# A weight ring of 16 chunks in place of 12, four windows in place of six, and the residual stream parked in DRAM, in a diffusion block with 32 experts

## The chip, the core and the metric

One core of one Trainium2 chip. Its engines are PE (TensorE, matmuls), DVE (VectorE), ACT (ScalarE), POOL (GpSimd) and SP (SyncE, here only an issuer of DMAs). The metric is the device time of one execution in microseconds.

## The reference, cut to what matters

A layer of a diffusion backbone over 512 tokens of 1024 channels: a mixer (Fourier heads and a gated linear recurrence), a gated residual, and then experts. Each token goes to 4 of 32 experts, each of which is a clamped SwiGLU with three float32 matrices of 1024 x 1024 (12.6 MB):

```python
logits = (hf @ w_router) + b_router
top_val, top_idx = lax.top_k(logits, TOP_K)          # 4 of 32
gates = jax.nn.softmax(top_val, axis=-1)
...
gu = xb @ w_gu[e] + b_gu[e]                           # 1024 -> 2048
gt = jnp.minimum(gu[:, :D_FF], SWIGLU_LIMIT)
up = jnp.clip(gu[:, D_FF:], -SWIGLU_LIMIT, SWIGLU_LIMIT)
act = (up + 1) * (gt * jax.nn.sigmoid(SWIGLU_ALPHA * gt))
out = act @ w_down[e] + b_down[e]                     # 1024 -> 1024
...
x = x + gt_f * moe_ffn(...)
return rmsnorm(x, g_final)
```

## The kernel before

All weights are float32 and are read once. The mixer and the router run up to about 310 us; then the experts run one after the other, each in one or more *items* of 64 token slots (`M`). The number of items of an expert follows from how many tokens chose it; for these inputs 32 experts make 45 items. The experts are sorted by their number of tokens and then put in a fixed order that spreads the big ones (`CST["place"]`): one of the eight biggest, then three smaller ones. An expert's number in this text is its place in that order, from 0, and items are counted from 0 too. Experts 0 to 31 have 2, 1, 2, 1, 2, 1, 1, 1, 3, 1, 1, 1, 2, 1, 1, 1, 4, 1, 2, 1, 2, 1, 1, 1, 2, 1, 1, 1, 2, 1, 1, 1 items. The table of items is worked out on the chip, so the loops over items take their numbers from registers: each engine has a loop of up to 63 turns (`NI`), of which those behind the last item do nothing.

The weights of an expert are 12 *chunks* (`NCH`) of 8 KB a partition, 1 MB each: 0 to 7 for gate and up, 8 to 11 for down. They go two steps:

1. SP loads chunk `c` of an expert into slot `c` of `ring` (`load_chunk`), when the chunk of the expert before has been copied out of that slot in that expert's last item (`wait_moved`). All of SP's loads stand in one queue. Chunks 0 to 7 are two DMAs each (L314), 8 to 11 one (L317).
2. In every item, each chunk is copied from the ring to one of the *windows*, which are typed for the matmul; window `c % NW`, with `NW` = 6. DVE copies chunks 0 to 5, 8 and 9 (`move`, L998), ACT 6, 7, 10 and 11 (`move`, L733). A copy waits until the chunk has landed (`w_loaded_c`) and until PE has used the chunk that lay in the window before (`slot_used`).

PE takes the chunks in order: `gate_up` (L1447) for 0 to 7, `down` (L1459) for 8 to 11; each is eight matmul instructions in the trace. An item opens with two bias matmuls (L1439). Between them stand transposes of the activations (L1469), of the gathered tokens of the next item (L1428) and small ones. DVE's turn for item `b` is: read the registers, pick the tokens of item `b + 2`, SwiGLU of the first half, numbers for the gather, copy 8, SwiGLU of the second half, copy 9, and then the copies 0 to 5 of item `b + 1`, which are waited for as PE frees the windows. ACT's turn: sigmoid, copies 6 and 7, a copy of activations, sigmoid, copy 10, activations, copy 11, and the output.

`xl` holds the residual stream (2 MB, 16 KB a partition) in SBUF from the mixer to the end. Behind the last item the sums of the experts' outputs are read back (`y_sb`), gated, added to `xl`, normalised and stored.

Of the kernel before, what the change touches and what calls it, by code (L numbers as in the profile page):

```python
# [5 lines left out]
F32 = mybir.dt.float32  # L6
# [4 lines left out]
ALU = mybir.AluOpType  # L11
# [3 lines left out]
P = 128  # L15
D = 1024
# [24 lines left out]
NW = 6  # L41
# [56 lines left out]
def build(nc, x, ctx, w_mod, b_mod, w_in, w_fourier, rg_w_a, rg_w_x, w_out, w_router, b_router,  # L98
          w_gate_up, bias_rows, w_down, g_norm_ffn, g_final, cols, cst, dft, out):
    h_dram = nc.dram_tensor("h_rows", (NL, D), F32, kind="Internal").ap()  # L100
    y_dram = nc.dram_tensor("y_rows", (NL * CG, YW), F32, kind="Internal").ap()

    with ExitStack() as stack:
# [107 lines left out]
        ring = at("ring", [P, NCH, CK, 2, HF], SLOT[0])  # L211
        window = [at(f"window_{i}", [P, CK, 2, HF], w) for i, w in enumerate((ZD, ZD + 8 * KB, ZD + 16 * KB, ZD + 24 * KB, ZA + 16 * KB, ZB))]
# [3 lines left out]
        gfin = at("gfin", [P, D], SLOT[3])  # L216
# [10 lines left out]
        o_sb = at("o_sb", [P, TL, D], SLOT[1])  # L227
        junk3 = at("junk3", [P, D], SLOT[2])
# [80 lines left out]
        def load_chunk(sp, c, e):  # L309
            h, k = c // 4, c % 4 * CK  # L310
            if h < 2:
                for g in range(2):
                    n0 = g * FF + h * HF
                    sp.dma_start(ring[:, c, :, g, :], wgu_v[e, :, k:k + CK, n0:n0 + HF]).then_inc(w_ld[c], 16)  # L314
            else:
                k = (c - 8) * CK
                sp.dma_start(ring[:, c, :, :, :].rearrange("p k g n -> p k (g n)"), wd_v[e, :, k:k + CK, :]).then_inc(w_ld[c], 16)  # L317

        def landed_at(c):
            return 32 if c < 8 else 16  # L320

# [35 lines left out]
        def _(sp):  # L357
# [44 lines left out]
            load_chunk(sp, 6, 0)  # L402
            load_chunk(sp, 7, 0)
# [3 lines left out]
            for c in range(4):  # L407
                load_chunk(sp, c, 0)
# [4 lines left out]
            load_chunk(sp, 4, 0)  # L413
            load_chunk(sp, 5, 0)
            sp.wait_ge(S["lg_done"], TL)
            load_chunk(sp, 10, 0)
            load_chunk(sp, 11, 0)
            sp.wait_ge(S["h_stored"], 16 * TL)
            sp.wait_ge(S["gathered"], 16)
            load_chunk(sp, 8, 0)  # L420
            load_chunk(sp, 9, 0)
# [23 lines left out]
            sp.wait_ge(S["stored"], 16 * TL)  # L445
# [115 lines left out]
        def _(act):  # L561
# [167 lines left out]
            def move(c, p, b):  # L729
                act.wait_ge(w_ld[c], landed_at(c) * p + landed_at(c))  # L730
                act.wait_ge(S["slot_used"], NCH * b + c - NW + 1)
                act.nop(nofuse=True)
                A(window[c % NW][:, :, :, :], ring[:, c, :, :, :], ACT.Copy).then_inc(S["moved_by_act"], 1)  # L733

# [25 lines left out]
            def square_out(t):  # L760
                act.wait_ge(S["x_out"], t + 1)
                if t:
                    act.wait_ge(S["ssq_out"], t)
                A(junk3[:, :], xl[:, t, :], ACT.Square, accum_out=ss[:, t:t + 1]).then_inc(S["ssq_out"], 1)
# [11 lines left out]
        def _(dve):  # L776
# [318 lines left out]
            dve.wait_ge(S["begin_done"], 1)  # L1095
            link(V.tensor_copy(place[:, 0:1], ps[0:NE, 4, 0:1]))
# [5 lines left out]
            V.tensor_scalar(table[:, 2 * NI:3 * NI], active[:, :], place[:, 3:4], None, ALU.mult)  # L1102
# [12 lines left out]
            V.memset(item_p[:, NI:], 0)  # L1115
# [6 lines left out]
            V.tensor_copy(item_p[:, 0:NI], ps[:, 5, 2 * NI:3 * NI])  # L1122
# [60 lines left out]
            dve.wait_ge(S["ld_gnf"], 32)  # L1183

            def add_y(t):
# [5 lines left out]
                V.tensor_tensor(xl[:, t, :], xl[:, t, :], y_sb[:, t, :], ALU.add).then_inc(S["x_out"], 1)  # L1191
# [5 lines left out]
            def scaled(t):  # L1197
                dve.wait_ge(S["rt_out"], t + 1)
                link(V.reciprocal(rsf[:, 1, t:t + 1], rsf[:, 1, t:t + 1]))
                V.scalar_tensor_tensor(o_sb[:, t, :], xl[:, t, :], rsf[:, 1, t:t + 1], gfin[:, :], ALU.mult, ALU.mult).then_inc(S["out_ready"], 1)  # L1200
# [337 lines left out]
```

## Time and profile before

| | |
|---|---|
| median of 3 runs | 1547.96 us (1547.79 to 1549.3) |
| profiled execution: its time | 1548.7 us |
| profiled execution: its span | 1546.8 us |
| busy: PE, DVE, ACT, POOL | 1352.8, 904.4, 639.3, 249.4 us |
| DMA from and to HBM | 463.07 MB read, 18.35 MB written |
| mean granted TensorE clock | 0.959 |

The times are of whole executions; the profile is of one of them, and its span leaves out what lies around the first and the last recorded event. Busy times are sums over the span: they don't say which engine sets the pace at a given place. That is read from stages, where one resource is full and another waits, and from the rows of the timeline, whose first two columns are start and duration in us. In brackets stand the idle time of the engine before the row and what ended it.

### The profile page before, as it was taken

Reading aid. Unit: us, or ns where it says so; the run is one execution under the profiler, and the core shown is the slowest. Engines: PE = TensorE matmul, PEld = TensorE weight load, DVE = VectorE, ACT = ScalarE, POOL = GpSimd, SP = SyncE. Lnnn points to the kernel's source line nnn. Section 1 sums busy time; section 2 is a strip of 40 time slices with the busy share of each in tenths; the row PEclk is TensorE's granted clock in tenths of the full one; section 3 lists DMA queues with packets and bytes.
Section 4 is the critical chain, followed back from the end, with each engine's and each line's share of the span. In section 5 each row is a group of like instructions: output and inputs, shape, how many; then the busy total and the mean of one; then the engine's idle time right before and its main releaser. Section 6 shows DMA issues by size and latency. Waiting matters only on the chain.

```text
span 1546.8 us, 23063 instructions
## 1 busy us (share of the span) xinstructions
PE 1352.8 (87%) x6259; PEld 538.8 (35%) x6259; DVE 904.4 (58%) x1452; ACT 639.3 (41%) x720; POOL 249.4 (16%) x156
## 2 busy tenths in 40 slices
PE   4798999489999987999789879999999779979981
PEld 2586567333333322333223223333333223323320
DVE  2999786855565544655456445656555456446546
ACT  3434552234354434444244434544445335335432
POOL 1741143211111101011001101111110011100101
PEclk9799999689999999999999999999999999999996
DMA  9656132739999999399999991699999999999993
GB/s 379 235 211 224 62 109 76 271 128 374 355 383 336 379 383 388 110 381 383 379 364 383 388 375 24 237 384 342 385 339 383 381 364 373 381 387 346 385 377 123
DMA packets 207171, 474.36 MB, mean 307 GB/s; under 512 B 18481, under 2 KB 18993, under 8 KB 206129
## 3 DMA queue, kind: packets, MB, share of 16 engines
q1 hardware_dynamic: 196322, 455.24, 79.6%
q0 software_dynamic: 10832, 18.90, 5.4%
q8 instruction: 9, 0.15, 0.0%
q14 instruction: 8, 0.07, 0.0%
HBM read 463.07 MB, written 18.35 MB: 311 GB/s over the span
## 4 chain that ended last, share of the span: by engine, by line
PE 34%; SPq 29%; DVE 15%; DMA 11%; issue 7%; ACT 3%; DVEq 1%; POOL 0%; ACTq 0%; POOLq 0%
SPq L314 22%; PE ps L1447 21%; PE ps L1459 7%; DMA ring<-in_w_down 6%; SPq L317 4%; DVE bc L845 4%; DMA ring<-in_w_gate_up 2%; DVE window L998 2%; DMA wm<-in_w_mod 2%; ACT window L733 2%; PE ps L1439 1%; PE ps L1325 1%; PE ps L1428 1%; DVE cv L861 1%; PE ps L1317 1%
## 5 line engine op out<-in xcount | busy, mean ns | idle before, releaser
L1447 PE MATMUL ps<-window,xT 128*64 128x512 f32 x2880 | 658.6, 605 | 45.9 <-DVE window L998 39.7
L998 DVE COPY window<-ring 128x2048 f32<-128x2048 f32 x366 | 438.1, 1226 | 211.8 <-DMA ring<-in_w_gate_up 167.8
L1459 PE MATMUL ps<-window,aT 128*64 128x512 f32 x1440 | 341.1, 603 | 20.9 <-DVE window L998 11.0
L733 ACT ACTIVATE window<-ring 128x2048 f32<-128x2048 f32 x180 | 337.9, 1900 | 48.5 <-DMA ring<-in_w_down 45.4
L1447 PEld LDWEIGHTS ps<-window,xT 128*64 128x64 f32 x2880 | 196.3, 138 | 438.7 <-issue 339.1
L727 ACT ACTIVATE sg<-gb 128x256 f32<-128x256 f32 x90 | 37.5, 417 | 491.8 <-DVE gb L1135 491.8
L540 POOL DMA_INDIRECT y_rows<-osb,idx_c x46 | 85.7, 1863 | 624.2 <-ACT osb L723 609.5
L1135 DVE TENSOR_SCALAR gb<-ps 128x256 f32<-128x256 f32 x90 | 38.1, 424 | 249.6 <-PE ps L1447 249.5
L1459 PEld LDWEIGHTS ps<-window,aT 128*64 128x64 f32 x1440 | 90.5, 136 | 178.0 <-issue 131.0
L527 POOL DMA_INDIRECT xg<-h_rows,idx_n x46 | 54.4, 1183 | 469.7 <-DVE idx_n L1028 469.7
L723 ACT ACTIVATE osb<-ps,gate_c 128x512 f32<-128x512 f32 x46 | 31.7, 689 | 112.3 <-PE ps L1459 111.7
L745 ACT ACT_TABLE_LOAD x45 | 57.7, 1283 | 12.2 <-issue 12.0
L1469 PE MATMUL ps<-csb,ab 128*128 128x128 f32 x180 | 40.3, 306 | 23.4 <-DVE ab L1142 23.4
L1439 PE MATMUL ps<-bias_w,pick 128*128 128x512 f32 x135 | 56.1, 470 | 0.7 <-ACT xT L716 0.7
L1469 PEld LDWEIGHTS ps<-csb,ab 128*128 128x128 f32 x180 | 18.4, 143 | 97.1 <-DVE ab L1142 69.5
L1013 DVE COPY metab<-meta 128x20 bf16 (+1 forms) x47 | 8.4, 178 | 70.5 <-issue 70.2
L1439 PEld LDWEIGHTS ps<-bias_w,pick 128*128 128x128 f32 x135 | 22.0, 190 | 73.1 <-issue 72.3
L1265 PE MATMUL ps<-hT_l_hi,win_hi 128*128 128x512 f32 x96 | 38.9, 405 | 6.3 <-DVE hT_l_lo L832 6.3
L716 ACT ACTIVATE xT<-ps 128x512 f32<-128x512 f32 x46 | 27.2, 591 | 33.5 <-PE ps L1428 33.5
L1428 PEld LDWEIGHTS ps<-csb,xg 64*128 64x128 f32 x368 | 26.8, 140 | 40.7 <-issue 40.7
L1142 DVE TENSOR_TENSOR ab<-ub,sg 128x256 f32<-128x256 f32 x90 | 38.3, 425 | 3.1
L1139 DVE SCALAR_TENSOR_TENSOR ub<-ub,gb 128x256 f32<-128x256 f32 x90 | 38.2, 425 | 3.1
(278 smaller groups left out, 1207.7 us busy)
## 6 DMA issues: line engine op xcount, KB each, us to landing
ring<-in_w_gate_up SPq DMA_DIRECT2D x512, 512.0 KB, 11.8
ring<-in_w_down SPq DMA_DIRECT2D x128, 1024.0 KB, 13.6
wm<-in_w_mod SPq DMA_DIRECT2D x4, 2048.0 KB, 21.5
wm_a<-in_w_mod SPq DMA_DIRECT2D x4, 2048.0 KB, 9.0
wm_b<-in_w_mod SPq DMA_DIRECT2D x4, 2048.0 KB, 8.7
win<-in_w_in SPq DMA_DIRECT2D x3, 2048.0 KB, 20.1
x_in<-in_x SPq DMA_DIRECT2D x1, 2048.0 KB, 10.4
wo_f<-in_w_out SPq DMA_DIRECT2D x1, 2048.0 KB, 7.5
```

Of the source, the lines that this page charges most:

```text
L314: sp.dma_start(ring[:, c, :, g, :], wgu_v[e, :, k:k + CK, n0:n0 + HF]).then_inc(w_ld[c], 16)
L317: sp.dma_start(ring[:, c, :, :, :].rearrange("p k g n -> p k (g n)"), wd_v[e, :, k:k + CK, :]).then_inc(w_ld[c], 16)
L527: pool.indirect_dma_start(xg[0:M, :], None, h_dram, bass.IndirectOffsetOnAxis(ap=idx_n[0:M, 0:1], axis=0), bounds_check=last_row, oob_is_e ...
L540: pool.indirect_dma_start(y_dram, bass.IndirectOffsetOnAxis(ap=idx_c[:, 0:1], axis=0), osb[:, :], None, bounds_check=last_part, oob_is_err ...
L733: A(window[c % NW][:, :, :, :], ring[:, c, :, :, :], ACT.Copy).then_inc(S["moved_by_act"], 1)
L745: A(table_kept[:, :], ones[:, 0:1], ACT.Sigmoid)
L845: ins = V.scalar_tensor_tensor(Z, W[:, k, :], csil[:, k, 0:1], Z, ALU.mult, ALU.add)
L998: V.tensor_copy(window[c % NW][:, :, :, :], ring[:, c, :, :, :]).then_inc(S["moved_by_dve"], 1)
L1439: return MMUL(ps[:, bank, :], pick[:, :], bias_w[:, bank * CH:(bank + 1) * CH], start=True, stop=False)
L1447: last = MMUL(ps[M * j:M * (j + 1), h, :].rearrange("m (g n) -> m g n", g=2), xT[:, k, :], window[c % NW][:, k % CK, :, j * GW:(j + 1) * G ...
L1459: last = MMUL(ps[M * y:M * (y + 1), 2, :], aT[:, h, i, M * j:M * (j + 1)], window[c % NW][:, k % CK, y, :], start=False, stop=(h == 1 and ...
L1469: last = nc.tensor.transpose(ps[:, 3, h * GW + i * P:h * GW + (i + 1) * P], ab[:, i * P:(i + 1) * P], ident)
```

## The change

The ring gets 16 slots (`NR`). Chunk `c` of expert `i` lies in slot `(12 i + c) mod 16`, a pattern that repeats after four experts (`PERIOD`), so SP's loop is written out for four experts and DVE and ACT work out the slot in a register (`ring_chunk`). The four further slots lie where `xl` and two of the six windows were. So the windows are four, DVE's copies 4 and 5 move from the end of an item's turn to the beginning of the next, and `xl` is stored to DRAM (`x2_dram`) once the first gather is done and loaded again (`x2`) when the second last expert has been copied out. SP also waits, before each load, that the load of the same chunk of the expert before has landed.

```diff
-NW = 6
+NW = 4
+NR = 16
+PERIOD = 4
...
-        def load_chunk(sp, c, e):
+        def load_chunk(sp, c, e, p):
             h, k = c // 4, c % 4 * CK
+            s = (NCH * p + c) % NR
...
+        def ring_chunk(c, p):
+            return ring[:, bass.ds((p * NCH + c) & (NR - 1), 1), :, :, :].rearrange("p s k g n -> p (s k) g n")
...
+            for t in range(TL):
+                sp.dma_start(x2_dram[t * P:(t + 1) * P, :], xl[:, t, :]).then_inc(S["stored"], 16)
+            load_chunk(sp, 8, 0, 0)
+            load_chunk(sp, 9, 0, 0)
...
-            with sp.Fori(1, NE) as i:
+            def load_expert(i, p, ahead, ahead_of_last):
                 e = sp.value_load(order_i[0:1, bass.ds(i, 1)], min_val=0, max_val=NE - 1)
-                before = sp.value_load(before_i[0:1, bass.ds(i, 1)], min_val=0, max_val=NI)
                 for c in range(NCH):
-                    wait_moved(sp, c, before)
+                    if c >= NR - NCH:
+                        wait_moved(sp, c - (NR - NCH), ahead)
+                    elif ahead_of_last is not None:
+                        wait_moved(sp, c + 2 * NCH - NR, ahead_of_last)
                     sp.nop(nofuse=True)
-                    load_chunk(sp, c, e)
-            sp.wait_ge(S["slot_used"], NCH * n)
+                    sp.wait_ge(w_ld[c], landed_at(c) * i)
+                    sp.nop(nofuse=True)
+                    load_chunk(sp, c, e, p)
+
+            sp.wait_ge(S["stored"], 16 * TL)
+            last = None
+            for p in range(1, PERIOD):
+                ahead = last_item_ahead_of(p)
+                load_expert(p, p, ahead, last)
+                last = ahead
+            with sp.Fori(1, NE // PERIOD) as r:
+                last = last_item_ahead_of(r * PERIOD - 1)
+                for p in range(PERIOD):
+                    ahead = last_item_ahead_of(r * PERIOD + p)
+                    load_expert(r * PERIOD + p, p, ahead, last)
+                    last = ahead
+            last = last_item_ahead_of(NE - 1)
+            wait_moved(sp, 9, last)
             sp.nop(nofuse=True)
-            sp.wait_ge(S["moved_by_dve"], len(BY_DVE) * n + NW)
+            wait_moved(sp, 11, last)
             sp.nop(nofuse=True)
+            load(x2[:, :, :], rows(x2_dram), "ld_x")
             load(gfin[:, :], g_final.partition_broadcast(P), "ld_gnf")
...
-                V.tensor_copy(window[c % NW][:, :, :, :], ring[:, c, :, :, :]).then_inc(S["moved_by_dve"], 1)
+                V.tensor_copy(window[c % NW][:, :, :, :], ring_chunk(c, p)).then_inc(S["moved_by_dve"], 1)
...
-            for c in range(4, NW):
-                move(c, 0)
-
...
                     def first_of_next(c):
-                        dve.wait_ge(S["slot_used"], NCH * b + NW + c + 1)
+                        dve.wait_ge(S["slot_used"], NCH * b + NCH + c - NW + 1)
                         move(c, p_next)
 
+                    second(4)
+                    second(5)
                     dve.wait_ge(S["meta_done"], b + 2)
                     pick_tokens(b + 2, e)
```

The rest of the diff gives `x2` the place of `xl` behind the experts, moves `gfin`, `o_sb` and `junk3`, puts one small DVE instruction into the table's making, and lets the entry behind the last item name the last expert. Below stand instructions in their order on an engine, with the line and the semaphores each waits for (`window_135` to `window_140` are windows 0 to 5).

DVE at the end of an item, before: copies 2 to 5 of the next item into the windows, and the jump back.

```order
L998 COPY window_137<-ring 128x2048 [waits w_loaded_2,slot_used]
L1162 REGISTER_ALU
L998 COPY window_138<-ring 128x2048 [waits w_loaded_3,slot_used]
L1162 REGISTER_ALU
L998 COPY window_139<-ring 128x2048 [waits w_loaded_4,slot_used]
L1162 REGISTER_ALU
L998 COPY window_140<-ring 128x2048 [waits w_loaded_5,slot_used]
L1152 UNCONDITIONAL_BRANCH
L1151 REGISTER_ALU
L1151 COMPARE_AND_BRANCH
```

DVE at the beginning of an item's turn, after: what stands now between the register reads and the token pick; L1188 and L1030 are the wait and the copy of chunks 4 and 5.

```order
L1029 ISA [waits slot_used]
L1030 ISA [waits w_loaded_4]
L1030 REGISTER_ALU
L1030 ISA
L1030 COPY window_135<-ring 128x2048
L1188 REGISTER_ALU
L1030 REGISTER_ALU [waits w_loaded_5,slot_used]
L1030 REGISTER_ALU
L1030 ISA
L1030 COPY window_136<-ring 128x2048
L1045 ISA [waits meta_done]
L1045 COPY metab<-meta 128x20
```

Copies 4 and 5 have moved across the loop's turn, stand ahead of the token pick and of the SwiGLU, and each has register instructions in front.

SP in the loop over experts, before: the first chunk of an expert and the wait of the second.

```order
L326 ISA
L314 ISA [waits moved_by_dve]
L314 DMA ring<-in_w_gate_up 128x2x512
L314 ISA
L314 DMA ring<-in_w_gate_up 128x2x512
L326 REGISTER_ALU
L314 ISA [waits moved_by_dve]
```

SP in the same place, after: the first chunk of the first of four experts (L446 is the index of the expert), and the second.

```order
L334 ISA
L446 REGISTER_ALU [waits moved_by_dve]
L319 ISA [waits w_loaded_0]
L319 DMA ring<-in_w_gate_up 128x2x512
L319 ISA
L319 DMA ring<-in_w_gate_up 128x2x512
L334 REGISTER_ALU
L319 ISA [waits moved_by_dve,w_loaded_1]
L319 DMA ring<-in_w_gate_up 128x2x512
L319 ISA
L319 DMA ring<-in_w_gate_up 128x2x512
L336 ISA
```

The wait for a copy now asks for chunks 8 and 9 of the expert two places back (`moved_by_dve`), and a second wait, for the landing of the same chunk of the expert before (`w_loaded_0`, `w_loaded_1`), has come with it.

## Rows read from the trace of the kernel before

**Rows 1.** By stage: busy us (count) of PE, PEld, DVE, ACT, POOL; clock, DMA share, GB/s.

```profile
485.00:627.00 142.00, 125.91 (x589) 40.45 (x587) 73.41 (x122) 57.09 (x61) 15.05 (x10) 0.99 1.02 369
...
627.00:650.00 23.00, 22.57 (x105) 7.24 (x103) 12.15 (x24) 12.28 (x13) 2.83 (x2) 1.00 0.10 14
...
650.00:792.00 142.00, 126.03 (x591) 40.52 (x589) 74.58 (x123) 56.48 (x61) 15.95 (x10) 0.99 1.03 371
...
792.00:930.00 138.00, 123.57 (x575) 39.59 (x571) 69.81 (x120) 56.81 (x60) 15.50 (x10) 0.99 1.03 375
...
930.00:978.00 48.00, 47.04 (x221) 15.51 (x222) 26.98 (x48) 24.20 (x26) 5.63 (x4) 1.00 0.11 17
...
1403.00:1509.00 106.00, 98.55 (x464) 32.32 (x460) 57.05 (x97) 46.22 (x51) 11.76 (x8) 0.98 1.00 367
```

**Rows 2.** Timeline of PE over one item (start us, us, what).

```profile
1031.30 0.74 PE L1439 MATMUL ps<-bias_w,pick 128*128 128x512 f32 x2
...
1032.06 10.52 PE L1447 MATMUL ps<-window,xT 128*64 128x512 f32 x48
...
1055.54 0.73 PE L1439 MATMUL ps<-bias_w,pick 128*128 128x512 f32 x2
```

**Rows 3.** Timeline of PE: the row that opens an item, at four of the five slow stretches.

```profile
562.42 0.73 PE L1439 MATMUL ps<-bias_w,pick 128*128 128x512 f32 x2
...
630.54 0.74 PE L1439 MATMUL ps<-bias_w,pick 128*128 128x512 f32 x2
...
868.22 0.74 PE L1439 MATMUL ps<-bias_w,pick 128*128 128x512 f32 x2
...
934.33 0.73 PE L1439 MATMUL ps<-bias_w,pick 128*128 128x512 f32 x2
...
1201.11 0.73 PE L1439 MATMUL ps<-bias_w,pick 128*128 128x512 f32 x2
...
1269.32 0.74 PE L1439 MATMUL ps<-bias_w,pick 128*128 128x512 f32 x2
...
1342.05 0.73 PE L1439 MATMUL ps<-bias_w,pick 128*128 128x512 f32 x2
...
1407.75 0.73 PE L1439 MATMUL ps<-bias_w,pick 128*128 128x512 f32 x2
```

**Rows 4.** Timeline of SP's queue: weight loads issued (start us, us, what, count).

```profile
315.21 0.88 SPq L317 DMA_DIRECT2D ring<-in_w_down  x2
...
339.16 17.65 SPq L314 DMA_DIRECT2D ring<-in_w_gate_up  x16
...
485.23 17.99 SPq L314 DMA_DIRECT2D ring<-in_w_gate_up  x16
...
789.24 19.77 SPq L314 DMA_DIRECT2D ring<-in_w_gate_up  x16
```

**Rows 5.** Timeline of ACT: the copy of expert 8's chunk 11.

```profile
626.71 1.91 ACT L733 ACTIVATE window<-ring 128x2048 f32<-128x2048 f32 x1 [0.29 <-DMA ring<-in_w_down]
```

**Rows 6.** DMA issues by tile: count, KB each, median us from issue to landing.

```profile
ring<-in_w_gate_up SPq DMA_DIRECT2D x512, 512.0 KB, 11.8
...
xl<-in_x SPq DMA_DIRECT2D x1, 2048.0 KB, 7.8
```

**Rows 7.** Costliest groups of the page: DVE's copies.

```profile
L998 DVE COPY window<-ring 128x2048 f32<-128x2048 f32 x366 | 438.1, 1226 | 211.8 <-DMA ring<-in_w_gate_up 167.8
```

**Rows 8.** What PE waited for, 317 to 1514 us: total, times, longest.

```profile
PE ps L1459 <- DVE window L998: 11.0, 45, 0.3
```

**Rows 9.** Timeline of DVE from the end of one item to the next.

```profile
1055.66 1.23 DVE L998 COPY window<-ring 128x2048 f32<-128x2048 f32 x1 [0.39 <-PE ps L1459]
1058.47 0.17 DVE L1013 COPY metab<-meta 128x20 bf16 x1 [1.58 <-issue]
```

**Rows 10.** Timeline of DVE behind the last item.

```profile
1526.29 3.06 DVE L1188 TENSOR_TENSOR y_sb<-y_sb,bc 128x1024 f32<-128x1024 f32 x1 [11.35 <-issue]
...
1533.79 1.23 DVE L1191 TENSOR_TENSOR xl<-xl,y_sb 128x1024 f32<-128x1024 f32 x1
```

More of the change, by code:

```diff
@@ L100, in build @@
     h_dram = nc.dram_tensor("h_rows", (NL, D), F32, kind="Internal").ap()
+    x2_dram = nc.dram_tensor("x2_rows", (NL, D), F32, kind="Internal").ap()
     y_dram = nc.dram_tensor("y_rows", (NL * CG, YW), F32, kind="Internal").ap()
@@ L209, in build @@
         table = at("table", [NE, 3 * NI + 2 * NE], RA + 8 * KB)
-        ring = at("ring", [P, NCH, CK, 2, HF], SLOT[0])
-        window = [at(f"window_{i}", [P, CK, 2, HF], w) for i, w in enumerate((ZD, ZD + 8 * KB, ZD + 16 * KB, ZD + 24 * KB, ZA + 16 * KB, ZB))]
+        ring = at("ring", [P, NR, CK, 2, HF], SLOT[0])
+        window = [at(f"window_{i}", [P, CK, 2, HF], w) for i, w in enumerate((ZD, ZD + 8 * KB, ZD + 16 * KB, ZD + 24 * KB))]
         xg = at("xg", [P, D], ZB + 16 * KB)
@@ L215, in build @@
         bias_w = at("bias_w", [P, 3 * CH], ZB + 8 * KB, F32R)
-        gfin = at("gfin", [P, D], SLOT[3])
+        gfin = at("gfin", [P, D], ZX + 8 * KB)
         osb = at("osb", [P, YW], ZB + 20 * KB)
@@ L226, in build @@
         y_sb = at("y_sb", [P, TL, D], SLOT[0])
-        o_sb = at("o_sb", [P, TL, D], SLOT[1])
-        junk3 = at("junk3", [P, D], SLOT[2])
+        x2 = at("x2", [P, TL, D], SLOT[1])
+        o_sb = at("o_sb", [P, TL, D], SLOT[2])
+        junk3 = at("junk3", [P, D], SLOT[3])
         zero = at("zero", [P, D], ZB + 18 * KB)
@@ L313, in load_chunk @@
                     n0 = g * FF + h * HF
-                    sp.dma_start(ring[:, c, :, g, :], wgu_v[e, :, k:k + CK, n0:n0 + HF]).then_inc(w_ld[c], 16)
+                    sp.dma_start(ring[:, s, :, g, :], wgu_v[e, :, k:k + CK, n0:n0 + HF]).then_inc(w_ld[c], 16)
             else:
                 k = (c - 8) * CK
-                sp.dma_start(ring[:, c, :, :, :].rearrange("p k g n -> p k (g n)"), wd_v[e, :, k:k + CK, :]).then_inc(w_ld[c], 16)
+                sp.dma_start(ring[:, s, :, :, :].rearrange("p k g n -> p k (g n)"), wd_v[e, :, k:k + CK, :]).then_inc(w_ld[c], 16)
         def landed_at(c):
             return 32 if c < 8 else 16
+        def ring_chunk(c, p):
+            return ring[:, bass.ds((p * NCH + c) & (NR - 1), 1), :, :, :].rearrange("p s k g n -> p (s k) g n")
         BY_DVE, BY_ACT = (0, 1, 2, 3, 4, 5, 8, 9), (6, 7, 10, 11)
@@ L401, in _ @@
             sp.wait_ge(S["pf_done"], TL)
-            load_chunk(sp, 6, 0)
-            load_chunk(sp, 7, 0)
+            load_chunk(sp, 6, 0, 0)
+            load_chunk(sp, 7, 0, 0)
             sp.wait_ge(S["ssr_done"], 1)
@@ L407, in _ @@
             for c in range(4):
-                load_chunk(sp, c, 0)
+                load_chunk(sp, c, 0, 0)
             for t in range(TL):
@@ L412, in _ @@
             sp.wait_ge(S["bias_ready"], 1)
-            load_chunk(sp, 4, 0)
-            load_chunk(sp, 5, 0)
+            load_chunk(sp, 4, 0, 0)
+            load_chunk(sp, 5, 0, 0)
             sp.wait_ge(S["lg_done"], TL)
-            load_chunk(sp, 10, 0)
-            load_chunk(sp, 11, 0)
+            load_chunk(sp, 10, 0, 0)
+            load_chunk(sp, 11, 0, 0)
             sp.wait_ge(S["h_stored"], 16 * TL)
             sp.wait_ge(S["gathered"], 16)
-            load_chunk(sp, 8, 0)
-            load_chunk(sp, 9, 0)
+            for t in range(TL):
+                sp.dma_start(x2_dram[t * P:(t + 1) * P, :], xl[:, t, :]).then_inc(S["stored"], 16)
@@ L444, in _ @@
                 sp.dma_start(out[t * P:(t + 1) * P, :], o_sb[:, t, :]).then_inc(S["stored"], 16)
-            sp.wait_ge(S["stored"], 16 * TL)
+            sp.wait_ge(S["stored"], 32 * TL)
         @block.gpsimd
@@ L732, in move @@
                 act.nop(nofuse=True)
-                A(window[c % NW][:, :, :, :], ring[:, c, :, :, :], ACT.Copy).then_inc(S["moved_by_act"], 1)
+                A(window[c % NW][:, :, :, :], ring_chunk(c, p), ACT.Copy).then_inc(S["moved_by_act"], 1)
             copy_xT(1)
@@ L763, in square_out @@
                     act.wait_ge(S["ssq_out"], t)
-                A(junk3[:, :], xl[:, t, :], ACT.Square, accum_out=ss[:, t:t + 1]).then_inc(S["ssq_out"], 1)
+                A(junk3[:, :], x2[:, t, :], ACT.Square, accum_out=ss[:, t:t + 1]).then_inc(S["ssq_out"], 1)
             def root_out(t):
@@ L1095, in _ @@
             dve.wait_ge(S["begin_done"], 1)
+            V.tensor_scalar(place[:, 2:3], place[:, 3:4], -(NE - 1.0), None, ALU.add)
             link(V.tensor_copy(place[:, 0:1], ps[0:NE, 4, 0:1]))
@@ L1101, in _ @@
             V.tensor_scalar(table[:, NI:2 * NI], active[:, :], place[:, 0:1], None, ALU.mult)
-            V.tensor_scalar(table[:, 2 * NI:3 * NI], active[:, :], place[:, 3:4], None, ALU.mult)
+            V.tensor_scalar(table[:, 2 * NI:3 * NI], active[:, :], place[:, 2:3], None, ALU.mult)
             V.tensor_scalar(table[:, 3 * NI:3 * NI + NE], const("expert")[0:NE, :], place[:, 3:4], const("index")[0:NE, :], ALU.is_equal, ALU.mult)
@@ L1114, in _ @@
             V.memset(item_o[:, NI:], 0.0)
-            V.memset(item_p[:, NI:], 0)
+            V.memset(item_p[:, NI:], NE - 1)
             dve.wait_ge(S["pick_ready"], 1)
@@ L1183, in _ @@
             dve.wait_ge(S["ld_gnf"], 32)
+            dve.wait_ge(S["ld_x"], 48)
             def add_y(t):
```

8 lines of the change are left out of this document (5 added, 3 removed).

## The prediction

> **What bounds the kernel now.** I read the busy time by stage first. While the experts run, two resources take turns at setting the pace. From 485 to 627 us the 16 DMA engines are busy all the time (share 1.02, 369 GB/s) and PE has 125.9 busy us of 142; from 627 to 650 DMA stands almost still (0.10, 14 GB/s) and PE is busy all through. 650 to 792 and 792 to 930 are DMA-full again, and 930 to 978 is empty [rows 1].
>
> The timeline of PE then gives the two paces. An item (64 token slots through one expert) that waits for nothing takes 1055.54 - 1031.30 = 24.24 us, and six chunks of it take 10.52 us, 1.75 us each [rows 2]. A chunk is 1024 KB, 1.05 MB: at 370 GB/s DMA needs 2.83 us for one, 34 us for the twelve of an expert. So an expert with one item is DMA's, and one with two items (48.5 us) is PE's. The order is a big expert, then three small ones, so DMA falls behind PE once in four experts. The rows that open items show it: 562.42 to 630.54 is two items and should be 48.5 us, it is 68.1 us; from 868.22 it is 66.1, from 1201.11 68.2, from 1342.05 65.7 [rows 3]. There are five such stretches; the one whose rows are left out lies between the first two of these, from 727 to 795, and is like the first. Excess in their order: 19.6, 19.6, 17.6, 19.7, 17.2, some 94 us in all. That is what a deeper ring can win from.
>
> When does DMA start on such a stretch? Chunk c of the next expert goes into the slot of chunk c of this one, so its load waits until that chunk has been copied to a window in this expert's last item. SP's queue issues expert 5's first load at 485.23, expert 1's at 339.16, though its last load before that left at 315.2 [rows 4]. DMA idles there because the ring is full, not because there is nothing to load.
>
> **The change, part by part.**
>
> *Ring 12 to 16.* Loads 4 to 11 of an expert now wait for chunks 0 to 7 of the one before, and loads 0 to 3 for chunks 8 to 11 of the one before that, long copied. So when an item releases the load that used to be chunk 0, chunks 0 to 3 are already there, provided DMA had four chunks' time to spare beforehand. All later landings of that DMA-full stretch come four chunks earlier: 4 x 1.05 MB at 370 GB/s = 11.3 us. Where is that spare time?
> - Stretch 485 to 627: DMA has nothing to do from the landing of the two chunks issued at 315.21 to 339.16, and is only paced by releases after that; the four chunks go in there and the lead is kept. Worth 11.3 us, below the excess of 19.6, so all of it is taken.
> - Stretch 650 to 930: it follows the hole 627 to 650, 23 us. Worth 11.3. It holds two slow stretches, but the second starts with no hole: its first load leaves at 789.24, when expert 12's last chunk is still on its way, and DMA is full on both sides of 792 [rows 1, 4]. A DMA that is never idle cannot be started earlier, so the second excess (17.6 us) stays.
> - From 978 on: it follows the hole 930 to 978. Worth 11.3 at the stretch that ends at 1269; the next (1342 to 1408) again follows without a hole and keeps its 17.2.
> Together 34 us. The last 106 us run at 367 GB/s against 375 from 792 to 930 [rows 1], from short waits for releases; with the lead they go: 106 x (1 - 367/375) = 2.3, I take 2. The time after expert 8's last chunk has landed (copied from 626.71, next item at 630.54 [rows 3, 5]) stays.
>
> *Windows 6 to 4.* A load is released by a copy, and a copy now waits for the chunk four back instead of six. For chunk 0 of the next item that is chunk 8 of this one; DVE comes to that copy only behind chunk 9's, so nothing is later. Copies 1 to 5 are 2 to 4 us later; the loads they release stand behind others in a queue that takes 11.8 us from issue to landing [rows 6], so DMA has work. Copies 6, 7, 10, 11 follow ACT's sigmoids as before. For PE: DVE's last copy of the old item starts at 1055.66, the loop's turn is over at 1058.47 [rows 9]; then chunk 4's copy (1.23 us [rows 7]) and chunk 5's, which waits for PE's chunk 1 (1055.54 + 0.76 + 2 x 1.75 = 1059.8) and ends at 1061.1; the token pick takes 0.9, so the SwiGLU can start at 1062.0. Its input is ready after four chunks, at 1063.3. Slack 1.3 us: cost nothing. If that cover were gone, each us would delay ACT's copy of chunk 6 and then PE.
>
> *Slot from a register.* Each of the 12 copies of an item gets three or four register instructions in front. They run beside the instruction ahead where that is long. The tight place is chunk 9's copy, which stands behind the SwiGLU's last product and for which PE already waits 0.24 us in each of 45 items [rows 8]. From the rows a register instruction costs 0.15 us or less: the loop's turn, some twenty of them, takes 2.81 us [rows 9]. Four are 0.6 at most, partly under the product (like its neighbours about 0.4 us long): 0 to 0.3 us an item. Only items on a PE-paced way to a DMA start count, some 15: 0 to 4.5, and I take 1, nearer to the end where they are hidden.
>
> *Residual stream.* The store of 2 MB goes ahead of chunks 8 and 9 of expert 0; the same size took 7.8 us as a load [rows 6]. They are wanted eight chunks, 14 us, into the first item: nothing. Without the cover it would be up to 8 us, once. The reload and g_final leave while the last expert runs and are wanted only behind the y_rows loads. DVE's end does not move: it waits out 11.35 us of skipped loop turns [rows 10], which are as many as before.
>
> Sum: -34 - 2 + 1 = -35 us. The profiled execution: span 1546.8, time 1548.7, so 1513.7; the median of the runs is 0.7 lower, so **1513.0 us**.
>
> The trace reads weights at 369 to 375 GB/s [rows 1]. The Trainium skill (DMA: Bandwidth & Descriptors, Specifications) puts a core's share of HBM at about 358 GB/s; by an estimate from that figure four chunks would be 11.7 us, three times that 35, and the sum 36. The trace is faster than the page, and I keep its rate.
>
> **Rivals.**
> - *Only two chunks net.* Ring and windows together held 18 chunks and hold 20. If the release of a load is what counts and it moves back with the windows, the lead is two chunks: -17 + 1, 1532 us. Against it: chunk 0's copy does not move. 6%.
> - *SP's long loop.* The loop over experts is now written out four times, some 250 instructions for some 60, and each load has a second wait. If SP's issue falls 2 us late at a DMA start, it costs 2 us there, 6 in three: 1519; it decides against the gain only from 12 us each. For it: nothing in the rows, SP is ahead of DMA by 11.8 us [rows 6] in the full stretches. 8%. The Trainium skill (Advanced Engine Details and Errata, ISA Cache) gives an engine two cache lines of 256 instructions; by that rule the new body could be fetched again on each turn, and no row here prices a fetch.
> - *Nothing.* DMA's holes are filled, but the excess moves to a later stretch: 1547 to 1549. Against it: the excess of each stretch is above 11.3 us, and PE-paced holes follow. 4%.
> - *Slower.* The copies run at 1.23 us for 2048 elements [rows 7], where an addition of two tiles takes 1.23 us for 1024 [rows 10]. If a copy with a source from a register falls to that pace, DVE's eight copies of an item take 9.8 us more. DVE is busy 26.98 us in 48 [rows 1], 13.5 an item; with 9.8 and the loop's turn of 1.6 it is at 24.9 without a single wait, and its waits for PE between them bring it to some 27. 45 items share 1197 us now [rows 8], 26.6 each: above that the kernel is slower. At 27 the loop takes 1215, 18 more: 1566 us. For it: no long copy in the kernel has such a source; `metab` has one, but 20 elements in 0.17 us tell nothing of a pace [rows 9]. Against it: shape, type and place of both tiles stay as they are. 5%.
>
> **Numbers.** Forecast 77% (own range 1507 to 1520: from -40, if also a us of stall in the first items and the slow start of the last item go, to -27, with 4.5 of register work and DMA starts 2 us late). With SP's rival the range 1506 to 1522 holds 84%. Faster by over 0.2% (3 us, about what this measurement can tell from no change): 77 + 6 + 8 = 91%; within it 4%; slower 5%.
>
> **What would show it.** Right: the two items from 562 us on no longer take 68 us, but one 24.2 and the other some 33; the stretch to 934 still loses two items' worth of 17 us; DMA busy between 317 and 345; copies at 1.23 us; PE's wait for chunk 9 at 0.24 to 0.34. Wrong if undisturbed items are above 24.4 us, if DMA's rate in full stretches is off 370 GB/s, or if SP's queue issues a first load more than 2 us behind the copy that releases it.

## The result, and the profile after

The change makes the kernel faster: 1523.67 us median (1520.89 to 1525.86, four runs) against 1548.63 for the kernel before on the same chip, a ratio of 0.9836 with a 95% interval of 0.9817 to 0.9856. That is 25 us where 35 were forecast, and just outside the range of 1506 to 1522. The profiled execution took 1525.86 us, its span is 1524.0, 22.8 shorter than that of before.

The page of the kernel after: the span, the DMA queue that fetches instructions, and three groups of instructions (DVE's copies are L1030 now, PE's matmuls L1480 and L1492).

```profile
span 1524.0 us, 25174 instructions
...
q14 instruction: 43, 0.35, 0.1%
...
L1480 PE MATMUL ps<-window,xT 128*64 128x512 f32 x2880 | 649.8, 599 | 38.9 <-DVE window L1030 23.4
L1030 DVE COPY window<-ring 128x2048 f32 (+1 forms) x364 | 445.0, 1228 | 343.3 <-DMA ring<-in_w_gate_up 109.2
L1492 PE MATMUL ps<-window,aT 128*64 128x512 f32 x1440 | 342.1, 604 | 32.1 <-DVE window L1030 21.9
```

A copy takes 1228 ns, as in [rows 7]: a source from a register does not slow it. PE's wait for DVE's windows ahead of L1492 has grown from 11.0 [rows 8] to 21.9 us; seven waits of 0.5 to 2.4 us, all in slow stretches, make 9 of it, and the others are 0.33 each. The line of q14 is the one that I had not thought to look at: 43 packets of 8 KB of instructions, where the page of before has 8.

Stage windows of the kernel after; the columns are those of [rows 1]. A *slow stretch* is one of the five pairs of items in which PE waits for DMA, a *hole* is a time in which DMA has nothing that it may load.

```profile
317.00:345.00 28.00, 26.98 (x121) 9.09 (x120) 13.54 (x25) 12.74 (x14) 3.47 (x2) 0.90 1.01 346
485.00:622.00 137.00, 126.65 (x603) 41.48 (x601) 75.06 (x123) 59.97 (x62) 15.64 (x10) 1.00 1.03 372
...
852.00:885.00 33.00, 25.18 (x117) 7.73 (x115) 13.16 (x23) 11.68 (x12) 2.79 (x2) 1.00 1.04 366
885.00:919.00 34.00, 25.68 (x117) 7.46 (x115) 16.75 (x26) 11.68 (x12) 3.61 (x2) 1.00 1.03 383
1319.00:1353.00 34.00, 26.28 (x115) 8.13 (x115) 14.01 (x24) 11.68 (x12) 3.18 (x2) 0.95 1.03 364
```

DMA is busy from 317 to 345 us (share 1.01), where SP used to have nothing it was allowed to load: the four chunks of lead go in there. The stretch to 622 still runs at 372 GB/s.

Timeline of PE after, the rows that open an item, at the first and the third slow stretch (the third row is cut at the end of the view):

```profile
563.36 0.73 PE L1472 MATMUL ps<-bias_w,pick 128*128 128x512 f32 x2
...
588.67 0.73 PE L1472 MATMUL ps<-bias_w,pick 128*128 128x512 f32 x2
...
622.75 0.50 PE L1472 MATMUL ps<-bias_w,pick 128*128 128x512 f32 x1
...
852.20 0.73 PE L1472 MATMUL ps<-bias_w,pick 128*128 128x512 f32 x2
...
885.09 0.73 PE L1472 MATMUL ps<-bias_w,pick 128*128 128x512 f32 x2
...
919.16 0.74 PE L1472 MATMUL ps<-bias_w,pick 128*128 128x512 f32 x2
```

The two items from 563.36 take 25.3 and 34.1 us, 59.4 in place of the 68.1 of [rows 3]: 8.7 won, not 11.3. The two from 852.20 take 67.0, 0.9 longer than before, where I had expected no change. Over all five stretches the same table gives 59.4, 59.1, 67.0, 59.3 and 68.1 us, in sum 23 less than before. So the lead arrives in the three stretches that were named, each a little short, and the two behind no hole have grown.

Where does it go? The chain of waits of SP in the kernel after, at the end of a turn of its loop (start us, us, what):

```profile
564.15 0.66 SPq L322
564.94 0.06 SPq L456
565.00 5.42 issue
570.42 0.07 SPq L456
...
572.83 0.38 SPq L319
```

L456 is the head of the loop over four experts. The turn ends at 564.94, then SP does nothing for 5.42 us, waiting for nothing that the profile shows, and the next load leaves at 572.83, some 8 us behind the last one. The trace shows the same at all six jumps back to the head: 5.2 to 5.4 us of nothing, 7.7 to 7.9 us between the loads. Fetches of instructions stand there and along the turn, five in each of seven turns, 35 of the 43.

### The profile page after: what moved, and what is told of

It reads as the page before. It is cut to its first block, busy times and chain, and to the rows that moved or that the text cites. A ratio compares the mean times of both kernels' runs of the same rounds, so it can differ in the third digit from the quotient of the medians.

```text
span 1524.0 us, 25174 instructions
## 1 busy us (share of the span) xinstructions
PE 1346.3 (88%) x6259; PEld 540.7 (35%) x6259; DVE 910.6 (60%) x1451; ACT 647.3 (42%) x720; POOL 254.8 (17%) x156
## 4 chain that ended last, share of the span: by engine, by line
PE 33%; SPq 30%; DVE 13%; DMA 11%; issue 10%; ACT 2%; DVEq 0%; POOL 0%; ACTq 0%; POOLq 0%
SPq L319 23%; PE ps L1480 18%; DMA ring<-in_w_down 7%; PE ps L1492 7%; SPq L322 5%; DVE bc L877 4%; DMA wm<-in_w_mod 2%; DVE window L1030 2%; ACT window L765 1%; PE ps L1472 1%; PE ps L1358 1%; PE ps L1382 1%; PE ps L1383 1%; PE ps L1384 1%; DMA ring<-in_w_gate_up 1%
## 5 line engine op out<-in xcount | busy, mean ns | idle before, releaser
L1480 PE MATMUL ps<-window,xT 128*64 128x512 f32 x2880 | 649.8, 599 | 38.9 <-DVE window L1030 23.4
L1030 DVE COPY window<-ring 128x2048 f32 (+1 forms) x364 | 445.0, 1228 | 343.3 <-DMA ring<-in_w_gate_up 109.2
L1492 PE MATMUL ps<-window,aT 128*64 128x512 f32 x1440 | 342.1, 604 | 32.1 <-DVE window L1030 21.9
L765 ACT ACTIVATE window<-ring 128x2048 f32 x180 | 339.9, 1908 | 58.1 <-DMA ring<-in_w_down 45.8
L1480 PEld LDWEIGHTS ps<-window,xT 128*64 128x64 f32 x2880 | 196.0, 137 | 422.5 <-issue 344.2
L572 POOL DMA_INDIRECT y_rows<-osb,idx_c x46 | 77.7, 1690 | 635.7 <-ACT osb L755 620.9
L1492 PEld LDWEIGHTS ps<-window,aT 128*64 128x64 f32 x1440 | 90.7, 136 | 189.3 <-issue 133.3
L559 POOL DMA_INDIRECT xg<-h_rows,idx_n x46 | 67.7, 1472 | 429.0 <-DVE idx_n L1060 429.0
L1299 PE MATMUL ps<-hT_l_lo,win_hi 128*128 128x512 f32 x96 | 38.4, 400 | 0.0
```

What stands on the lines that cost most here:

```text
L559: pool.indirect_dma_start(xg[0:M, :], None, h_dram, bass.IndirectOffsetOnAxis(ap=idx_n[0:M, 0:1], axis=0), bounds_check=last_row, oob_is_e ...
L572: pool.indirect_dma_start(y_dram, bass.IndirectOffsetOnAxis(ap=idx_c[:, 0:1], axis=0), osb[:, :], None, bounds_check=last_part, oob_is_err ...
L765: A(window[c % NW][:, :, :, :], ring_chunk(c, p), ACT.Copy).then_inc(S["moved_by_act"], 1)
L1030: V.tensor_copy(window[c % NW][:, :, :, :], ring_chunk(c, p)).then_inc(S["moved_by_dve"], 1)
L1480: last = MMUL(ps[M * j:M * (j + 1), h, :].rearrange("m (g n) -> m g n", g=2), xT[:, k, :], window[c % NW][:, k % CK, :, j * GW:(j + 1) * G ...
L1492: last = MMUL(ps[M * y:M * (y + 1), 2, :], aT[:, h, i, M * j:M * (j + 1)], window[c % NW][:, k % CK, y, :], start=False, stop=(h == 1 and ...
```

## The experiments

Ratios are to the kernel before, run on the same chip, with their 95% interval. "The change" stands at 0.9836. The theories for the missing 10 us: A, SP's loop is fetched again at each turn, and the time in which it issues nothing makes the DMA-full stretches longer; B, the register instructions ahead of the copies; C, four chunks of lead are worth only 8 us. F came up after the first runs: the written-out form, or the cadence of SP's issues, costs in another way than by fetches. Instructions in a turn are counted as the trace shows them executed: 430 in the change, 94 before.

**Is it SP's long loop?** The loop of one expert again, with the slot of a load from a register:

```diff
-            with sp.Fori(1, NE // PERIOD) as r:
-                last = last_item_ahead_of(r * PERIOD - 1)
-                for p in range(PERIOD):
...
+            load_expert(1, last_item_ahead_of(1), None)
+            with sp.Fori(2, NE) as i:
+                load_expert(i, last_item_ahead_of(i), last_item_ahead_of(i - 1))
...
+                    load_chunk_at(sp, c, e, bass.ds((i * NCH + c) & (NR - 1), 1))
```

> The change with one thing taken back: SP's loop holds one expert again (12 chunks, as before the change), and the ring slot of a load is worked out in a register; waits, lead and windows as in the change. Theory A: the loop of four experts is fetched again at each turn, SP issues nothing for some 8 us there and each DMA-full block loses about 2 us, so five blocks give back 10 us: 1514, the two slow blocks behind no hole no longer grow, and the instruction queue's bytes fall back to the 0.07 MB of before. Theory B: register instructions ahead of the copies cost the missing 10 us: 1524, as the change. Theory C: four chunks of lead are worth only 8 us each: 1524 too.

Measured: 1516.52 us, ratio 0.9765 (0.9748 to 0.9781), 11 us better than the change. Timeline of SP's queue in the change:

```profile
560.42 4.40 SPq L322 DMA_DIRECT2D ring<-in_w_down  x4
572.83 22.34 SPq L319 DMA_DIRECT2D ring<-in_w_gate_up  x16
```

And in short_loop, with its line of q14 and two of its stage windows:

```profile
q14 instruction: 9, 0.07, 0.0%
```

```profile
561.42 4.12 SPq L332 DMA_DIRECT2D ring<-in_w_down  x4
568.50 26.59 SPq L329 DMA_DIRECT2D ring<-in_w_gate_up  x16
```

```profile
850.00:883.00 33.00, 26.76 (x129) 8.43 (x127) 13.19 (x24) 12.56 (x14) 3.04 (x2) 1.00 1.05 380
1314.00:1347.00 33.00, 26.08 (x120) 8.01 (x117) 14.15 (x24) 11.84 (x13) 2.56 (x2) 1.00 1.05 380
```

The first load of the next expert leaves 4.3 us earlier, 3 us behind the last down load in place of 8, and where the change has 366 and 364 GB/s (852 to 885, 1319 to 1353), this one has 380: the last expert of a stretch lands sooner. Its five slow stretches are 58.9, 58.2, 65.0, 58.6 and 65.0 us, 7 less in sum than the change's. The hypothesis fits. It does not yet tell a refetch from other things that the written-out form brings.

**Does the place of the loop matter?** Waits that are met already, put where SP waits anyway, move the loop to other addresses (48 here, 160 in the second):

```diff
+            for _ in range(48):
+                sp.wait_ge(S["lg_done"], TL)
+                sp.nop(nofuse=True)
             sp.wait_ge(S["h_stored"], 16 * TL)
```

> The change with 48 more instructions on SP, ahead of its loops, where SP waits for h_stored anyway (waits that are met already); the loop of four experts is the same, 430 instructions, but begins 48 further on. The trace of the change shows five fetches of 8 KB in each turn. If what SP holds is four pieces of 8 KB (128 instructions of 64 bytes), the loop touches five pieces where it stands and four here: the fetches end and the time is that of short_loop, ratio 0.976 to 0.978 of before. If it holds two pieces of 16 KB, three are touched in both places: as the change, 0.984. If the unrolling costs by something else than its place: 0.984 too.

> As shift48, with 160 instructions: the loop then touches four pieces of 8 KB and two of 16 KB, so by both of these it fits, the fetches end, and the ratio is 0.976 to 0.978. If the refetch is not what costs, or if the unrolled loop costs by its length: 0.984.

Measured: 0.9854 (0.9838 to 0.9870) and 0.9822 (0.9802 to 0.9842); the fetches stay, 50 and 46 packets. Both simple pictures of what SP holds fall, as far as the place of a loop can be counted from executed instructions (no view shows its address); that the cost stays where the fetches stay fits the refetch but does not prove it.

**Length and form.** The same four experts with the wait for the landing carried by the instruction behind it, and short_loop with two and with four experts in a turn:

```diff
                     sp.wait_ge(w_ld[c], landed_at(c) * i)
-                    sp.nop(nofuse=True)
                     load_chunk(sp, c, e, p)
```

> The change with SP's loop of four experts made shorter: the wait for the landing (w_loaded) is carried by the instruction behind it and no longer stands in an instruction of its own, so the trace should show 382 instructions in a turn in place of 430; every wait, load, slot and order is as in the change. before_sp4 had 370 in a turn and no fetches. Theory A, the refetch is what costs: few or no fetches here and a ratio of 0.976 to 0.979 of before, as short_loop. Rival F, the written-out form costs in another way, or short_loop gains by the other cadence of its issues: 0.983 to 0.985. If the fetches stay, nothing is told apart.

> short_loop with two experts in a turn, some 270 instructions, slots from a register. Theory A: no fetches, ratio 0.975 to 0.978 as short_loop. Rival F with the written-out form at fault: between short_loop and the change, 0.979 to 0.982.

> short_loop with four experts in a turn, some 535 instructions, slots from a register as in short_loop. Theory A: five or more fetches in each of seven turns, as in the change, and 0.983 to 0.985. Rival F with the cadence of register slots as the gain: 0.975 to 0.978, whatever is fetched.

Measured: trim 0.984 (0.9824 to 0.9855), and it is still fetched (43 packets), so it does not separate A from F. It shows something else: SP stands still twice at each of its six jumps, and 12.2 to 12.9 us pass between the loads where the change has 7.7 to 7.9, and yet the time is that of the change. So the loss does not simply grow with the silence. dyn2 0.9775 (0.9759 to 0.9792), dyn4 0.9856 (0.9838 to 0.9874). Their lines of q14, dyn2 first:

```profile
q14 instruction: 10, 0.08, 0.0%
```

```profile
q14 instruction: 50, 0.41, 0.1%
```

The two have the same loads, slots and register work for each expert, and differ in how many experts stand in a turn: the long one loses some 12 us and is refetched. The cadence of register slots is not the gain.

**The refetch in the kernel before.** One part of the change by itself (the loop written out four times, 370 instructions in a turn), and then with 16 met waits for each expert (434 in a turn), with the short loop and the same waits as control (110):

```diff
+            for i in range(1, 4):
+                load_expert(i)
+            with sp.Fori(1, NE // 4) as r:
+                for k in range(4):
+                    load_expert(r * 4 + k)
```

```diff
+                for _ in range(16):
+                    sp.wait_ge(S["table_ready"], 1)
+                    sp.nop(nofuse=True)
```

> The kernel before with one part of the change: SP's loop over experts is written out four times, ring, windows and waits as before. Theory A: the refetch costs some 2 us in each of five DMA-full blocks, 1555 to 1559. Theories B and C: SP is ahead of DMA, so nothing, 1548 to 1550.

> The kernel before with 16 waits that are met already ahead of each expert's loads on SP, 110 instructions in a turn. Control for before_sp4_waits: 1.000 to 1.002 by every theory, no fetches.

> before_sp4 with the same 16 waits for each expert: 434 instructions in a turn of four experts in place of 370, nothing of the change besides. Theory A: SP's loop is fetched again in each of seven turns, five times 8 KB or more, and costs 7 to 10 us against before_waits: ratio 1.005 to 1.007. Rival F, something of the change other than the refetch goes with the fetches: fetches, but 1.000 to 1.002. If no fetches come, the length is not what brings them.

Measured: before_sp4 0.9999 (0.9986 to 1.0013), a miss for theory A as I had put it; but its page has 13 packets on q14, so 370 instructions are not fetched again and there was nothing to pay. before_waits 0.9986 (0.9974 to 0.9997). before_sp4_waits 1.0051 (1.0033 to 1.0069), 10 us above its control. The page's q14 line and SP's timeline of before_sp4_waits:

```profile
q14 instruction: 43, 0.35, 0.1%
```

```profile
571.08 5.25 SPq L317 DMA_DIRECT2D ring<-in_w_down  x4
584.72 20.33 SPq L314 DMA_DIRECT2D ring<-in_w_gate_up  x15
```

And the timeline of before_waits:

```profile
570.94 4.94 SPq L317 DMA_DIRECT2D ring<-in_w_down  x4
578.81 25.49 SPq L314 DMA_DIRECT2D ring<-in_w_gate_up  x16
```

The same waits cost nothing in a short loop and 10 us in a long one, and the long form without them (before_sp4) costs nothing either, in a kernel with the ring, windows and slots of before: the cost comes with the refetch. SP's first load leaves 13.6 us after the last expert's down loads began, 7.9 in the control.

**Register slots and windows.** Three parts in the kernel before: slots from a register, four windows, both.

```diff
+            return ring[:, bass.ds((p * 16 + c) & 15, 1), :, :, :].rearrange("p s k g n -> p (s k) g n")
```

```diff
-NW = 6
+NW = 4
...
+                    second(4)
+                    second(5)
```

> The kernel before with one part of the change: the ring slot of DVE's and ACT's copies in the experts' loop comes from a register, with the same slots as before. Theory A: 0.09 us for an item that waits for nothing and 0.25 us more of PE's wait for chunk 9, on some 15 PE-paced items: 1550 to 1552. Theory B: this is where the 10 us went: 1557 or more.

> The kernel before with one part of the change: four windows in place of six, with copies 4 and 5 at the turn's start. In the change an item that waits for nothing takes 24.33 us (24.24 before) and PE's wait for chunk 9 has doubled, and before_reg showed neither. So the windows should: 24.33 us for an item here, 1550 to 1553 us. If it was the register work together with the windows, this one shows 24.24 and 1547 to 1549.

> The kernel before with four windows and with slots from a register, both together; each by itself left an item at 24.24 us and the time within 0.1%. If the two together make the 24.33 us of the change: 24.33 here, PE's wait for chunk 9 doubled, and 1552 to 1555 (ratio 1.001 to 1.004). If neither: 24.24, and the 0.09 us comes from the ring's place or the loop's other parts.

Measured: 1.0001 (0.9988 to 1.0014), 1.0004 (0.9995 to 1.0013), 1.0000 (0.9990 to 1.0011); an item stays at 24.24 us in all three. But the first and the third did not do what I had said: (p*16+c)&15 has been folded into c in the built program, and no copy in them has a register instruction for its slot. They are repeats of the kernel before and of before_nw4, and show only that the windows cost nothing measurable. A form that keeps the registers, with a zero that is read at run time:

```diff
+        def slot_of(c, z):
+            return ((z * 4 + c) & 15) if c < 8 else ((z * 3 + c) & 11)
```

> The kernel before, with ring slots that really come from a register: in before_reg the build had folded (p*16+c)&15 into c, and its copies had no register instruction in front. Here each copy of the loop has the same three in front as in the change, and the same slots as before. The change's trace says 0.09 us an item, before chunk 9's matmuls. Theory A: 24.33 us for an item that waits for nothing, PE's wait for chunk 9 at 0.33, and 1 to 4 us in all: ratio 1.000 to 1.003. Theory B (the missing 10 us are register work): 1.006.

Measured: 1.0063 (1.0039 to 1.0087). That is theory B's figure, and both mechanisms that I had named for it are wrong: an item stays at 24.24 us and PE's wait for chunk 9 at 0.25. Timeline of PE, the first matmuls of chunk 9, in the change, in before_nw4_reg (no register instruction for the slot) and in before_reg2:

```profile
1010.40 1.94 PE L1492 MATMUL ps<-window,aT 128*64 128x512 f32 x8 [0.33 <-DVE window L1030]
```

```profile
1000.10 1.94 PE L1461 MATMUL ps<-window,aT 128*64 128x512 f32 x8 [0.24 <-DVE window L1001]
```

```profile
1005.70 1.94 PE L1469 MATMUL ps<-window,aT 128*64 128x512 f32 x8 [0.25 <-DVE window L1006]
```

So three register instructions hide under the SwiGLU's last product, and the change, where the wait for the window needs a fourth, pays 0.09 us an item: 24.33 in place of 24.24. Where before_reg2 loses its time is in the slow stretches. In its page by stage the granted clock falls there:

```profile
597.00:632.00 35.00, 27.76 (x117) 8.26 (x115) 18.89 (x29) 11.64 (x12) 4.30 (x2) 0.90 0.84 310
729.00:765.00 36.00, 28.20 (x117) 8.36 (x115) 14.76 (x25) 11.68 (x12) 4.26 (x2) 0.91 1.05 381
```

The five stretches sum to 342.7 us against 338.9 in before_waits. That is 4 of some 9 us; the rest is not in its one profile. The clock does not explain the 4 by itself, for before_waits shows 0.95 in six of the ten items of its slow stretches; the cause stays open.

**What a chunk of lead is worth.** The wait of a load moved back to the chunk it stood on before (lead 0), in the change and in short_loop, and to two chunks:

```diff
-                    if c >= NR - NCH:
-                        wait_moved(sp, c - (NR - NCH), ahead)
-                    elif ahead_of_last is not None:
-                        wait_moved(sp, c + 2 * NCH - NR, ahead_of_last)
+                    wait_moved(sp, c, ahead)
```

> The change, but each load waits for the copy of the same chunk of the expert before, as ahead of the change: the ring's four more slots are there and give no lead, all else (long loop, register slots, four windows, second wait, residual stream in DRAM) stays. Its distance to the kernel before is the price of all the rest. Theory A and B: 10 to 13 us above before, 1559 to 1562, and the lead is worth 35 to 38. Theory C: the rest costs 3 at most, 1549 to 1552, and the lead is worth 25 to 28.

> short_loop without the lead: each load waits for the copy of the same chunk of the expert before. Its distance to before is the price of windows, register slots, second wait and store without the refetch; its distance to short_loop is what the lead is worth. Theory A (the refetch is 10 of lead0's 12 us): ratio 1.000 to 1.003, and the lead is worth 36 to 40. Rival: the 12 us of lead0 come from the second wait or from the other parts: 1.006 to 1.008, and the lead is worth 46.

> short_loop with a lead of two chunks in place of four. short_lead0 stands at 1.006 and short_loop at 0.9765, 46 us for four chunks, more than the 34 of the sum: some 34 to 37 are the lead in three DMA-full stretches, the rest short waits at the start of an expert that any lead covers. If so two chunks cover these and give half the lead: 0.986 to 0.989. If each chunk is worth the same 11.5 us: 0.991.

Measured: lead0 1.0073 (1.0059 to 1.0087), short_lead0 1.0060 (1.0044 to 1.0076), short_lead2 0.9871 (0.9853 to 0.9890). By short_loop's 0.9765 the third and fourth chunks of lead are worth 0.0106, 16.4 us, 2.7 us for a chunk in each of three stretches. That is near DMA's pace, and theory C falls. The first two are worth 0.0189, 29 us, 13 more than the next two. The profiles say where. Rows that open and end the first slow stretch, short_lead2 and then short_loop:

```profile
561.10 0.73 PE L1474 MATMUL ps<-bias_w,pick 128*128 128x512 f32 x2
...
625.25 0.74 PE L1474 MATMUL ps<-bias_w,pick 128*128 128x512 f32 x2
```

```profile
562.98 0.73 PE L1474 MATMUL ps<-bias_w,pick 128*128 128x512 f32 x2
...
621.88 0.73 PE L1474 MATMUL ps<-bias_w,pick 128*128 128x512 f32 x2
```

The stretch takes 64.2 and 58.9 us. The third and fourth chunks shorten it and the two others behind a hole by 5.2, 5.9 and 6.7 us, and the two without a hole not at all (64.8 and 64.7 us, then 65.0 and 65.0). The first two chunks (short_lead0 against short_lead2) shorten all five, by 2.5 to 4.2 us each.

short_lead0 missed theory A's 1.000 to 1.003 and came out in its rival's 1.006 to 1.008: without a lead the other parts of the change cost 9 us with no refetch at all. before_reg2 later gave the same 1.006 with the register slots alone. In short_lead0's trace six items at the start of an expert also take 25.1 to 25.9 us where 24.33 is the rule, 7 us in sum, and none does so in short_lead2 or short_loop. I read this so: without a lead each load is waited for as soon as it is released, and any lead covers that. lead0 is refetched and yet only 2 us above short_lead0: its slow stretches are 8 us longer in sum, and its experts' starts 5 shorter. So in this pair the refetch costs 2 us and not 10; what makes the starts shorter is open.

## Why the prediction was off

*What held.* The reading of the two paces, and that DMA idled because the ring was full. The three stretches that win, and the two behind no hole that win little: 65.0 and 65.0 us in short_loop, 66.1 and 65.7 in [rows 3]. The refetch-free kernels made from before show 66.1 to 68.8 there, and short_lead0 67.6 and 67.5, so a lead may be worth 2 us there after all, but two chunks give as much of it as four. DMA busy from 317 to 345. Copies at 1.23 us. Windows six to four at nothing: before_nw4 at 1.0004. Nothing for the residual stream: the first item takes 26.6 us where it took 26.3. The end: from the last slow stretch on the change is 2.4 us shorter, with 2 forecast, though from the last item's start on kernels of one kind differ by up to 3 us.

*The term of the leads.* 11.3 us each from 370 GB/s was of the right size: by the timed runs the third and fourth chunks are worth 2.7 us each in a stretch, 2.83 was used. In the profiles all four together are worth less: in short_loop the three stretches are 9.2 to 9.8 us shorter than in before, 28.6 in sum for the 34 forecast. The two spans are 31 us apart and the ratio says 36, so single profiles say less of it than the timed runs.

*The step that failed.* "SP's long loop" was a rival at 8% and not a term of the sum. Its length was miscounted, some 250 instructions for some 60, where the trace executes 430 for 94. It stood at nothing with "nothing in the rows" for it and the 11.8 us of queue ahead [rows 6] against it. The rival was priced as 2 us at each of three DMA starts. What the runs showed is another place and a larger sum: at each of six jumps SP issues nothing for some 8 us (3 in short_loop), most of the queue that it was ahead by, and in the DMA-full stretches the rate falls from 380 to 365 GB/s about it. Against short_loop the two slow items of the change are 0.5 to 0.9 us longer in the three stretches behind a hole, and 2 and 3 us in the two that follow another without one, where DMA has been full over one jump more. The cost is 0.9836 less the mean of short_loop and dyn2, 0.9770: 10 us. Taken away, the time is 0.9770 x 1548.6 = 1513 us, the time that was forecast.

That the missing 10 us come with the refetch is shown from both sides: dyn2 against dyn4 in the changed kernel (12 us), before_waits against before_sp4_waits in the kernel before (10 us). How a pause of SP becomes lost time is argued and not shown: trim pauses longer and loses no more, and without a lead the changed kernel loses 2 us by it.

*Luck.* That the rest then meets the forecast to a microsecond is in part chance. Two terms are off and cancel: without a lead the other parts of the change cost 9 us (short_lead0), where the sum had 1, and from there the leads and what else they cover are worth 46 us, where it had 36.

The Trainium skill (Advanced Engine Details and Errata, ISA Cache), which the prediction cited for two cache lines of 256 instructions, pointed at the right thing. By an estimate from its figures, though, 382 and 430 instructions would fit into the two lines if they began well, and by my count the loop moved by 160 did begin well; it was fetched again all the same. The runs decide: 370 instructions in a turn were not fetched again, 382, 430, 434 and 535 were.

*The register term.* Taken as 1 us with a bound of 4.5. Its visible part in the change is 0.09 us on the 34 items outside the slow stretches, 3 us, inside the bound. Alone in the kernel before, three such instructions for each copy cost some 9 us (before_reg2), of which 4 are seen in the stretches where DMA sets the pace and none in the tight place that I had costed. With the lead this does not show in the sum, but no run takes the register slots away and keeps the lead.

## What to carry to other kernels

Before writing a loop out to make a ring's slots constants, count the instructions of one turn on the engine that issues the loads, and look at the instruction queue's packets on the page: here a body that was fetched again stopped its engine for 5 us at each jump, and a queue that was 12 us ahead did not hide that while DMA was full. A slot worked out in a register keeps the loop short; its own cost with a lead was not measured, but the kernels that have it and a short loop are the best here: short_loop at 0.9765 and dyn2 at 0.9775, which are the same within their intervals.

More lead is worth about its transfer time once for each hole that is followed by a DMA-full stretch, and nothing in a stretch that follows without a hole. The first chunks of lead are worth more than that, for they also cover short waits elsewhere (29 us for two chunks, 16 for the next two). And an experiment that puts a value in a register should be looked at in the built order of instructions first: two of these had folded it into a constant.

## What the hardware showed that I had not expected

- SP's instructions were fetched in pieces of 8 KB, five or six in a turn of the loops that did not stay. At each jump came one pause of 5.2 to 6.1 us and 7.7 to 8.9 us between loads (trim: two pauses, 12.2 to 12.9 us); in the loops that stayed it was 1.9 to 3.0 us.
- Neither a first instruction 48 nor one 160 further on changed that, and the limit seen lies between 370 and 382 executed instructions, in loops that begin within a few instructions of each other.
- The granted clock, 1.00 in items that wait for nothing, falls to 0.90 to 0.95 in some of the slow ones, where PE waits 8 us and more for chunks; PE's busy time in them then rises from 25.6 to 27 or 28 us. It is one of its two levels, 1.2 GHz, for part of the item. The item that opens the fifth slow stretch (1342 to 1376 us) has 0.95 in the kernel before and 1.00 in before_waits.
